# Expert blocks of 64 rows on two column halves of the array, with weights loaded once and copied on chip

## What is computed

```python
def _moe(h, router_w, router_b, w1, w3, w2):       # h: 512 x 1024
    s = sigmoid(t @ router_w)                       # 512 x 16
    # 4 groups of 4 experts: the best group by its two best scores, and in it the two best experts
    gates = ...                                     # two nonzero weights in a row, their sum 1
    for e in range(16):                             # w1[e], w3[e]: 1024 x 256, w2[e]: 256 x 1024
        hid = silu(t @ w1[e]) * (t @ w3[e])
        y = y + gates[:, e:e + 1] * (hid @ w2[e])
```

## Time and profile before

| | |
|---|---|
| median of 3 runs | 1456.61 us (1454.08 to 1458.19) |
| span of the profiled execution | 1449.7 us |
| PE busy | 1305.1 us, 90% of the span |
| DVE busy | 748.0 us, 52% |
| ACT busy | 347.5 us, 24% |
| POOL busy | 244.6 us, 17% |
| moved by DMA | 247.25 MB, mean 171 GB/s |

### The profile page before, as it was taken

One profiled execution on the slowest core, in us unless ns is written; L12 is line 12 of the kernel. 1 busy time (PEld: TensorE's weight loads), 2 busy tenths in 40 slices (PEclk: granted clock), 3 DMA queues, 4 the chain that ended last, 5 costly groups with the idle time before them and its releaser, 6 DMA issues.

```text
span 1449.7 us, 22238 instructions
## 1 busy us (share of the span) xinstructions
PE 1305.1 (90%) x8266; PEld 854.6 (59%) x8266; DVE 748.0 (52%) x1474; ACT 347.5 (24%) x786; POOL 244.6 (17%) x262
## 2 busy tenths in 40 slices
PE   2989999998999999799999699999999996999990
PEld 2578867656444444585843577777786454444440
DVE  5677573754222233878336567777764234222224
ACT  4000146002211110101058434433432012111111
POOL 0000047000110002100002423333333000010003
PEclk9899899897999999899999799999999997999995
DMA  9677555654799996311110000000003123899985
GB/s 367 197 262 288 188 203 204 225 181 163 236 343 358 361 364 232 131 70 47 59 58 1 31 2 2 20 2 2 2 2 117 58 77 126 290 352 351 336 292 217
DMA packets 128851, 247.25 MB, mean 171 GB/s; under 512 B 8208, under 2 KB 78048, under 8 KB 128768
## 3 DMA queue, kind: packets, MB, share of 16 engines
q1 hardware_dynamic: 116496, 203.04, 40.7%
q0 software_dynamic: 7056, 25.69, 4.9%
q10 hardware_dynamic: 5216, 17.36, 3.0%
HBM read 218.28 MB, written 27.79 MB: 170 GB/s over the span
## 4 chain that ended last, share of the span: by engine, by line
PE 56%; DMA 24%; DVE 11%; issue 4%; ACT 2%; SPq 1%; POOL 1%; POOLq 0%; DVEq 0%; ACTq 0%
DMA WR<-in_moe_w 21%; PE PS L2047 13%; PE PS L2013 8%; PE PS L1968 5%; PE PS L2185 3%; PE PS L2329 2%; PE PS L2378 2%; PE PS L1941 2%; PE PS L2266 2%; DMA arena<-in_ada_w 2%; PE PS L2360 2%; DVE arena L1314 2%; PE PS L2117 1%; PE PS L2445 1%; SPq L726 1%
## 5 line engine op out<-in xcount | busy, mean ns | idle before, releaser
L2185 PE MATMUL PS<-WR,arena 128*128 (+1 forms) x528 | 233.5, 595 | 11.6 <-ACT arena L1130 6.3
L2185 PEld LDWEIGHTS PS<-WR,arena 128*128 128x128 f32 x528 | 97.7, 190 | 125.4 <-issue 121.5
L1570 DVE TENSOR_TENSOR arena<-arena,PS 128x256 f32<-128x256 f32 x33 | 13.9, 421 | 207.2 <-ACT arena L1143 178.8
L2047 PE MATMUL PS<-WR,arena 128*128 128x256 f32 x480 | 111.7, 393 | 4.3 <-DVE arena L1692 4.2
L2013 PE MATMUL PS<-WR,arena 128*128 128x512 f32 x256 | 112.3, 595 | 0.0
L2204 PE MATMUL PS<-W,arena 128*128 x248 | 111.9, 592 | 0.0
L2047 PEld LDWEIGHTS PS<-WR,arena 128*128 128x128 f32 x480 | 94.2, 198 | 20.3 <-DVE arena L1692 3.4
L1314 DVE SCALAR_TENSOR_TENSOR arena<-arena,cact 128x1024 f32<-128x1024 f32 x77 | 99.6, 1294 | 12.4 <-DMA arena<-in_ada_w 6.5
L1968 PE MATMUL PS<-arena,WR 128*128 128x512 f32 x192 | 86.0, 604 | 1.1 <-DVE arena L1401 1.1
L2013 PEld LDWEIGHTS PS<-WR,arena 128*128 128x128 f32 x256 | 48.1, 191 | 56.2 <-issue 56.2
L864 POOL TENSOR_TENSOR LO<-GB,tmp 128x256 f32<-128x256 f32 x80 | 68.0, 870 | 71.2 <-DVE GB L1766 56.9
(11 more groups left out here) (375 smaller groups left out, 2129.0 us busy)
## 6 DMA issues: line engine op xcount, KB each, us to landing
WR<-in_moe_w SPq DMA_DIRECT2D x66, 1024.0 KB
arena<-in_ada_w SPq DMA_DIRECT2D x82, 512.0 KB, 4.6
W<-in_moe_w SPq DMA_DIRECT2D x33, 1024.0 KB
expert_rows<-arena ACTq DMA_DIRECT2D x31, 512.0 KB, 7.5
WR<-in_rwkv_w_rkv SPq DMA_DIRECT2D x6, 2048.0 KB, 8.5
WR<-in_mix_w_in SPq DMA_DIRECT2D x5, 2048.0 KB, 10.0
WR<-in_mix_w_out SPq DMA_DIRECT2D x2, 2048.0 KB, 7.9
expert_rows<-arena SPq DMA_DIRECT2D x1, 4096.0 KB, 14.6
```

The source lines that it names most:

```text
L2047: last = mm(out[:, n * 256:n * 256 + 256], left, right, start=(c == 0), stop=(c == 3))
L2185: last = mm(PS[:, 2, :], XgT[:, c, :], WR[:, slot, c, :].rearrange("p s f -> p (s f)"), start=(c == 0), stop=(c == KC - 1))
```

## The change

- Items become blocks of 64 rows (`ROWS`), up to 32, worked in pairs: everything for a block stands in buffer 0 or 1. If the number of blocks is odd, one is added.
- A gather reads half rows: partitions 0 to 63 get the first 512 columns of 64 rows, partitions 64 to 127 the second. Four transposes turn a block in place of eight.
- Weights of an expert are loaded once, by SP, into a ring of four slots of 6144 columns (`expert_slots`), in the order of the experts. The arena's areas are renumbered (`AT`) so that six lie together for the ring; four experts are loaded before the list is there. SP tells of an expert that has landed by a semaphore of its own (`landed`).
- For each block DVE and ACT copy the expert's weights from its slot to fixed tiles (`stage_up`, `stage_down`). The slot comes from the expert's number, which each of the two engines reads from `CN` into a register.
- `up` and `down` give each half of the array its own columns: with 64 rows in the stationary operand, half `h` writes PSUM partitions 64 h to 64 h + 63 and has its own moving columns.
- ACT does silu, a copy of weights and the scaling for the other block of the pair in one order, DVE another, both below.

```diff
+ROWS = 64
+MAX_ITEMS = 32
+SLOTS = 4
+        AT = (0, 4, 5, 1, 2, 3, 6, 7)
+        expert_slots = arena[:, 2:8, :].rearrange("p a n -> p (a n)").rearrange("p (s f) -> p s f", s=SLOTS)
+        UP_DVE, DOWN_DVE = 2560, 1024
...
@@ SP
+                def load(e):
+                    slot = expert_slots[:, e % SLOTS, :]
+                    for k, name in enumerate(("moe_w1", "moe_w3", "moe_w2")):
+                        sp.dma_start(slot[:, k * 2048:(k + 1) * 2048].rearrange("p (c f) -> p c f", c=2 if k == 2 else KC),
+                                     io[name][layer, e].rearrange("(c p) f -> p c f", p=P)
+                                     ).then_inc(sem(f"ring_in{e % SLOTS}"), 16)
+                def landed(e):
+                    sp.wait_ge(sem(f"ring_in{e % SLOTS}"), 48 * (e // SLOTS + 1 + layer * NEXP // SLOTS))
+                    sp.sem_inc(sem("landed"), 1)
...
+                load(0)
                 sp.wait_ge(*full("y", 8 * layer + 8))
+                load(1)
+                landed(0)
+                if layer == 0:
+                    sp.wait_ge(*full("mod", 5))
+                load(3)
+                landed(1)
                 sp.wait_ge(sem("xn"), NB * (2 * layer + 2))
+                sp.dma_start(xn_dram.rearrange("(b p) f -> p b f", p=P), XN).then_inc(sem("rows_out"), 16)
+                sp.wait_ge(sem("rows_out"), 16 * layer + 16)
+                load(2)
+                sp.wait_ge(sem("items"), layer + 1)
...
+                for e in range(SLOTS, NEXP):
+                    copied = sp.value_load(CN[0:1, 40 + e - SLOTS:41 + e - SLOTS], min_val=1, max_val=MAX_ITEMS)
+                    for engine in "va":
+                        sp.wait_ge(M(f"staged_{engine}"), copied * 2 + 1)
+                    load(e)
+                    if e > SLOTS:
+                        landed(e - 1)
...
@@ ACT
+                def stage_up(n, e):
+                    act.wait_ge(sem("landed"), e)
+                    nc.scalar.copy(up_stage[n][:, UP_DVE:UP], expert_slots[:, bass.ds((e + 3) % SLOTS, 1), UP_DVE:UP]
+                                   ).then_inc(M("staged_a"), 1)
+                def pair(at, k, first=False, final=False):
+                    silu(0, at(2))
+                    if not final:
+                        ahead = expert(k + 2)
+                        stage_up(0, ahead)
+                    turned(1, at(3))
+                    if not first:
+                        row_out(1, k - 1, at(4))
+                    stage_down(1, expert(k + 1))
+                    silu(1, at(4))
+                    if not final:
+                        stage_up(1, expert(k + 3))
+                        turned(0, at(5))
+                    row_out(0, k, at(6))
+                    if not final:
+                        stage_down(0, ahead)
...
@@ DVE
+                def pair(at, sent, k, first=False, final=False):
+                    hidden(0, at(2))
+                    turned(1, at(3))
+                    hidden_T(0, at(2))
+                    if not final:
+                        ahead = expert(k + 2)
+                        stage_up(0, ahead)
+                    if not first:
+                        scaled(1, at(0), sent[1])
+                    stage_down(1, expert(k + 1))
+                    hidden(1, at(4))
+                    if not final:
+                        turned(0, at(5))
+                    hidden_T(1, at(4))
+                    if not final:
+                        stage_up(1, expert(k + 3))
+                    scaled(0, at(2), sent[0])
+                    if not final:
+                        stage_down(0, ahead)
...
@@ PE
+                def up(n, turned, staged):
+                    pe.wait_ge(M("xga_sil"), turned)
+                    pe.wait_ge(M("xgv_hid"), turned)
+                    pe.wait_ge(M("staged_a"), staged)
+                    pe.wait_ge(M("staged_v"), staged)
+                    w = up_stage[n].rearrange("p (m c f) -> p m c f", m=2, c=KC)
                     for c in range(KC):
+                        for h in range(2):
+                            last = mm(PS[rows2[h], 2 + n, 0:2 * P].rearrange("p (m f) -> p m f", m=2), XgT[:, n, c, :],
+                                      w[:, :, c, cols(h)], start=(c == 0), stop=(c == KC - 1))
+                    last.then_inc(M("tx_up"), 1)
+                def pair(at, landed, first=False, final=False):
+                    up(0, at(1), 1 if first else at(0))
+                    turn(1, landed[1])
+                    if not first:
+                        down(1, at(0), at(1), at(0))
+                    turn_hidden(0, at(2))
+                    up(1, at(3), at(2))
+                    if not final:
+                        turn(0, landed[0])
+                    down(0, at(2), at(3), at(2))
+                    turn_hidden(1, at(4))
```

More of the change, by code:

```diff
@@ L923, in moe @@
+                for n in range(2):
+                    gather(n, n, first=True)
+                    gp.reg_mov(indexed[n], n + 3)
+                    gp.reg_mov(taken[n], 2 * n + 1)
+                gp.reg_mov(gathered, 0)
+                with gp.Fori(1, pairs_of) as i:
                     gp.reg_add(gathered, gathered, 16)
-                    gp.indirect_dma_start(Xg, None, xn_dram, src).then_inc(M("xg_in"), 16)
+                    for n in range(2):
+                        gather(n, i * 2 + n)
@@ L1147, in moe @@
[L1147 to L1155 removed]
+                act.wait_ge(sem("items"), layer + 1)
@@ new lines, in moe @@
+                act.wait_ge(sem("rest_out"), 16)
+                stage_up(0, expert(0))
+                turned(0, 1)
+                stage_up(1, expert(1))
+                stage_down(0, expert(0))
+                pair(lambda d: d, 0, first=True)
+                for d in step:
+                    act.reg_mov(step[d], d + 4)
+                with act.Fori(0, pairs_of - 2) as i:
+                    pair(counted, i * 2 + 2)
+                    for d in step:
+                        act.reg_add(step[d], step[d], 4)
@@ L2221, in moe @@
-                pe.wait_ge(M("hT"), n)
-                pe.wait_ge(M("w2_in"), n * 16)
-                for half in range(2):
-                    for c in range(2):
-                        last = mm(PS[:, half, :], hidL[:, c, :],
-                                  W2[:, bass.ds((n + 1) % 2, 1), c, half * 512:half * 512 + 512].rearrange("p s f -> p (s f)"),
-                                  start=(c == 0), stop=(c == 1))
-                    last.then_inc(M("down" if half else "th"), 1)
+                pe.wait_ge(sem("items"), layer + 1)
@@ new lines, in moe @@
+                keep_warm(PS[:, 5, :], 5)
+                turn(0, 16)
+                pair(lambda d: d, [32, 16], first=True)
+                for d in step:
+                    pe.reg_mov(step[d], d + 4)
+                pe.reg_mov(landed[0], 48)
+                pe.reg_mov(landed[1], 32)
+                with pe.Fori(0, pairs_of - 2) as i:
+                    pair(counted, landed)
+                    for d in step:
+                        pe.reg_add(step[d], step[d], 4)
+                    for n in range(2):
+                        pe.reg_add(landed[n], landed[n], 16)
```

486 lines of the change are left out of this document (215 added, 271 removed).

## The result

The changed kernel takes 1567.89 us (median of 4 runs, 1561.54 to 1570.05), the kernel before, on the same chip, 1457.4 (1454.08 to 1458.2): a ratio of 1.0767, 95% interval 1.0735 to 1.0799. It is 7.7% slower where 1.2% faster was forecast, and it lies outside the range.

The account below looks back on a forecast made before the run. TensorE and DMA were taken as overlapping limits before; afterwards chains through ACT and DVE set the stages. Terms -16.1 - 8.8 + 6.5 + 1 = -17.4 us gave span 1432.3, time 1439; range 1400 to 1490.

Parts of the forecast that it names:

- DMA: Expert stages: 50 MB of weights and rows a layer, 144 us at 349 GB/s, hidden at 7.7 us a block.
- the 181 of the chain: Expert stage of each layer: 3.65 + 11 x 15.36 + 5.3 + 3.3 = 181 us, against 197.1 and 189.8 before.
- weight loads never the last to arrive: Sign expected in the profile of the expert stages if the forecast held; no size given.
- start of layer 0: Before the first up product: normed rows queue behind expert 3's load, +5 us, and TensorE's lower clock, +1.5 us.
- The second chain: Down product, DVE's copies and output scaling, ACT's store, read and down copy, next silu and up: 15.36 us a pair.
- rival 1: Register reads hidden behind ACT's and DVE's work (0.3 us or less): about 165 us a layer, 1407 us; chance 0.2.
- rival 2: Ahead of ACT's and DVE's copies: issue costs over 0.8 us; gain gone at 1.04, 1475 at 1.3 us; chance 0.2.
- rival 3: DVE's up copy at the slow rate, 2.86 for 1.56 us: +15.6 us a layer, 1470 us; chance 0.07.
- rival 4: Up product's halves do not overlap: TensorE needs 11.2 us a block, 1615 us; 0.04 given for this and the next.
- rival 5: Weight loads stand between the up product's matmuls: up 5.8 us, 1526 us; 0.04 given for this and the previous.
- rival 6: Nothing changes: waits at the start and the ring eat the gain, 1456 us; chance 0.04.
- the rule of the Trainium skill that the prediction quotes: TensorE's up product: a weight load overlaps a running matmul only where row groups differ; would make up 5.8 us.

Follow-up runs that it names:

- the run into one region: Changed kernel with its row store still one DMA, aimed at one contiguous 256 KB per block (rows misplaced for the gathers): 1436.51 us.
- two DMAs of 64 partitions: Changed kernel with each block's row store issued by ACT as two 64-partition DMAs instead of one: 1478.75 us, ratio 1.0178 to the kernel before.
- The kernel with the rows stored first: Changed kernel with the row store split in two DMAs and SP storing the normed rows before loading expert 3: 1466.1 us, ratio 1.0094.

## Why the prediction was wrong

**The step that failed** is the one headed *DMA*: "50 MB, 144 us at 349 GB/s. It is hidden at 7.7 us a block". It divided the bytes by the rate of a stretch in which the DMA engines are at 0.88, as if every DMA used all of them. The bytes were right, the division was not: the row store, 0.26 MB of them a block, goes to two engines, and the last to finish counts. For these two the estimate is 246 us instead of 144, more than the 181 of the chain, and the stages measure 237 and 238. No rival held this case; I asked what each queue issues and when, never on how many engines one DMA runs. The line "weight loads never the last to arrive" was the check that showed it.

**The rest, read on the run into one region**, in which only that is mended:

| term | predicted | measured |
|---|---|---|
| up product, 32 instructions | 3.65 us | 3.67 |
| ACT's copies; DVE's up copy | 1.50, 1.05; 1.56 | 1.47, 1.05; 1.50 |
| silu's start to ACT's copy, first and second of a pair | 0.80, 0.80 | 0.81, 0.17 |
| store issue | 0.4 | 0.34 |
| two blocks | 15.36 | 14.70 |
| TensorE waits per block | 1.1 | 0.86 to 1.07 |
| stages | 181, 181 | 181.2, 180.5 |
| start of layer 0; stretch between the stages; end | +6.5, +1, 0 | +6.9, +1.8, +1.3 |
| span against 1449.7 | -17.4 | -15.3 |

That the stages agree to a microsecond is partly luck, for two errors cancel. The second chain is 0.66 us a pair shorter, nearly all of it the read after the second silu, which I had put at 0.80 and which is hidden; and two or three blocks a layer come 1 to 3 us late (at the first loop, and for weights in layer 0). So rival 1 is true for one of ACT's three reads a pair, and out for the two others: after the first silu, and between store and down copy (441.86 to 442.67). Rivals 2 to 6 are out: no read at 1.04 us or more, DVE at the fast rate, halves overlapping, no loads between products, and a time of 1568 us, or of 1436 with one region. On the loads the measurement decides against the rule of the Trainium skill that the prediction quotes: at 379.94 us in the changed kernel 32 loads for all rows cover 2.2 us and the products by themselves 3.4, and together they take 3.67.

Outside the stages the changed kernel loses 17 us against the one with one region (11.1 + 9.1 instead of 1.8 + 1.3), and the traces point to the same cause. After a stage POOL waits for the last row stores before it combines (its L924, in the changed kernel and in the one with one region):

```profile
L924 POOL DMA_INDIRECT arena<-expert_rows,SLI x16 | 15.3, 959 | 87.5 <-DMA expert_rows<-arena 83.3 <-issue 4.3
```

```profile
L924 POOL DMA_INDIRECT arena<-expert_rows,SLI x16 | 15.7, 978 | 60.4 <-DMA expert_rows<-arena 56.1 <-issue 4.3
```

27 us more for two layers; some of it overlaps other work.

**Why two DMAs of 64 partitions cost 42 us more than one.** The stages are 38.0 us longer. ACT's issues take 1.16 us a block instead of 0.34, in the second chain, and a pair at full clock takes 15.5 us instead of 14.7: 0.8 x 24 = 19 us. The rest is TensorE's clock. The kernel with the rows stored first, TensorE and its granted clock:

```profile
426.34 5.36 PE L2274 MATMUL PS<-WR,arena 128*64 128x256 f32 x32 [1.84 <-ACT arena L1146]
...
435.27 3.67 PE L2274 MATMUL PS<-WR,arena 128*64 128x256 f32 x32 [0.85 <-ACT arena L1146]
...
443.69 5.36 PE L2274 MATMUL PS<-WR,arena 128*64 128x256 f32 x32 [1.84 <-ACT arena L1146]
```

```profile
443.80:447.00 3.20, 3.20 (x16) 1.85 (x18) 1.81 (x3) 0.56 (x1) 0.00 (x0) 0.50 1.06 367
447.00:449.00 2.00, 2.00 (x19) 1.08 (x15) 0.00 (x0) 0.48 (x1) 0.00 (x0) 0.95 1.11 350
```

After an idle time of 1.84 us these up products begin at 0.50, 1.2 GHz, and take 1.69 us longer; after 0.85 the one between begins at full speed. It is not so every time: of the 19 up products of this run that follow 1.83 to 1.84 us of idle, 13 are slow and 6 are not; of the 22 after 0.74 to 1.25 us, none is slow. What decides it for the 19, no run here tests. From first to last start, 17 of 48 up products take over 3.6 us in the run with two DMAs, together 28.4 us above the 3.29 of the quickest; with one region it is 4 and 8.2 us. 19 + 20.2 = 39 us, against the 38.0. I had put this in at the start alone.

## What to carry to other kernels

Read each DMA's outermost dimension, on both sides (the runs here varied the target alone) and after what can be merged, before dividing bytes by a rate: one small store on two engines held up weight loads twelve times its size. Spread it, by another layout in DRAM or by two DMAs, and look per queue at how many engines run, since a DMA share of 0.6 with everything waiting for DMA is what this looks like. On an engine that copies ahead, put what the very next product needs before what is needed two blocks later: the same instructions in that order gave 50 us.

## What the runs showed of the hardware that I had not expected

- The number of engines of a DMA from ACT follows the outermost dimension: at most 2.1, 4.1 and 15.7 at work for 2, 4 and 16, and 2, 4 and 16 packets of 4 bytes for each.
- Its issue on ACT follows the pattern and not the number of engines: 0.53, 0.55 and 0.56 us for 2, 4 and 16, 0.34 for one region, 1.03 for the half rows of the changed kernel.
- A pause of 1.84 us before an up product was followed by 1.2 GHz in 13 of 19 cases, one of 0.74 to 1.25 us in none of 22; where it happens, 0.8 us more on ACT costs 2.5 us in a block.
- The narrow pattern costs 89 us against two DMAs from ACT (1567.89 and 1478.75), and 39 us from POOL (1430.67 and 1391.72), in a kernel that also scales first.
